# Seven-product units of a Hymba block: one of four column sums moved from VectorE to an adding transfer issued by GpSimd

## What is computed

```python
D_MODEL, SEQ, D_FF = 2048, 256, 5632
def swiglu(x, w_gate, w_up, w_down):
    return (jax.nn.silu(x @ w_gate) * (x @ w_up)) @ w_down
h = h + 1/2 * swiglu(rms_norm(h, ffn1_norm), w_gate1, w_up1, w_down1)
u = rms_norm(h, mix_norm) @ w_in          # split into attention and RWKV-7 columns
h = h + concat([dsa_attention(...), rwkv7_time_mix(...)]) @ w_out
h = h + 1/2 * swiglu(rms_norm(h, ffn2_norm), w_gate2, w_up2, w_down2)
return rms_norm(h, final_norm)
```

## Time and profile before

| what | value |
|---|---|
| median of 3 runs | 1834.93 us (1834.79 to 1837.94) |
| span of the profiled execution | 1834.2 us |
| median less that span | 0.7 us |
| TensorE busy | 1819.6 us, 99% |
| VectorE busy | 1505.4 us, 82% |
| ScalarE busy | 995.2 us, 54% |
| GpSimd busy | 11.1 us, 1% |
| HBM read | 360.19 MB |

### The profile page before, as it was taken

The page is one execution under the profiler, slowest core; times in us unless marked ns, Lnnn a source line. Parts: engine busy times, 40 slices in busy tenths (PEclk is TensorE's granted clock), DMA queues, the critical chain, the costliest instruction groups (busy, mean ns, idle before and its releaser), DMA issues. The chain is left out here.

```text
span 1834.2 us, 29749 instructions
## 1 busy us (share of the span) xinstructions
PE 1819.6 (99%) x10696; PEld 1546.4 (84%) x10696; DVE 1505.4 (82%) x1755; ACT 995.2 (54%) x1181; POOL 11.1 (1%) x23
## 2 busy tenths in 40 slices
PE   9999999999999999999999999999999999999998
PEld 7888888888888888999998878888888888888886
DVE  5888888888988985788867866688888888889996
ACT  7555555545555655754535655545555555555554
POOL 1000000000000000000000000000000000000000
PEclk9999999999999999999999999999999999999999
DMA  7677666777766778564443557677777677676664
GB/s 252 221 219 228 219 216 215 220 229 236 233 202 204 225 224 267 173 184 140 138 116 106 176 171 261 180 232 231 229 224 232 216 227 222 217 240 195 209 208 157
DMA packets 207851, 380.36 MB, mean 207 GB/s; under 512 B 16016, under 2 KB 35728, under 8 KB 207504
## 3 DMA queue, kind: packets, MB, share of 16 engines
q1 hardware_dynamic: 206768, 377.08, 65.7%
q10 hardware_dynamic: 480, 1.97, 0.3%
q0 software_dynamic: 512, 0.06, 0.0%
HBM read 360.19 MB, written 18.87 MB: 207 GB/s over the span
## 5 line engine op out<-in xcount | busy, mean ns | idle before, releaser
L402 ACT CAST whi<-raw 128x1024 fp32r<-128x1024 f32 (+1 forms) x648 | 675.1, 1047 | 700.8 <-DVE raw L1476 189.6
L411 DVE TENSOR_TENSOR wlo<-raw,whi 128x1024 fp32r<-128x1024 f32 (+1 forms) x648 | 771.7, 1212 | 208.4 <-ACT whi L402 194.5
L428 PE MATMUL psA<-whi,xh 128*128 128x512 f32 (+1 forms) x572 | 219.5, 384 | 0.5 <-DVE wlo L411 0.5
L428 PE MATMUL psA<-whi,xl 128*128 128x512 f32 (+1 forms) x572 | 219.2, 383 | 0.0
L428 PE MATMUL psA<-wlo,xh 128*128 128x512 f32 (+1 forms) x572 | 219.1, 383 | 0.0
L428 PE MATMUL psB<-whi,xh 128*128 128x512 f32 x544 | 211.7, 389 | 0.0
L428 PE MATMUL psB<-wlo,xh 128*128 128x512 f32 x544 | 211.6, 389 | 0.0
L428 PE MATMUL psB<-whi,xl 128*128 128x512 f32 x544 | 211.6, 389 | 0.0
L428 PEld LDWEIGHTS psA<-whi,xh 128*128 128x128 f32 x572 | 107.4, 188 | 21.6 <-DVE wlo L411 0.7
L428 PEld LDWEIGHTS psA<-whi,xl 128*128 128x128 f32 x572 | 107.4, 188 | 21.2
L428 PEld LDWEIGHTS psA<-wlo,xh 128*128 128x128 f32 x572 | 107.4, 188 | 21.0
(11 more groups left out here) (520 smaller groups left out, 3447.3 us busy)
## 6 DMA issues: line engine op xcount, KB each, us to landing
raw<-in_ffn_w_gate SPq DMA_DIRECT2D x176, 512.0 KB, 4.5
raw<-in_ffn_w_up SPq DMA_DIRECT2D x176, 512.0 KB, 4.6
raw<-in_ffn_w_down SPq DMA_DIRECT2D x176, 512.0 KB, 4.6
raw<-in_w_in SPq DMA_DIRECT2D x80, 512.0 KB, 3.6
raw<-in_w_out SPq DMA_DIRECT2D x32, 512.0 KB, 4.2
quads_dram<-stage SPq DMA_DIRECT2D x88, 128.0 KB, 4.2
stage<-quads_dram SPq DMA_DIRECT2D x22, 512.0 KB, 4.3
x<-in_x SPq DMA_DIRECT2D x4, 512.0 KB, 7.5
```

Source lines behind the costliest of these rows:

```text
L402: nc.scalar.copy(whi[:, slot, :, 0:ncol], raw[:, slot, :, 0:ncol]).then_inc(hi_ready, 1)
L411: nc.vector.tensor_tensor(wlo[:, slot, :, 0:ncol], raw[:, slot, :, 0:ncol], whi[:, slot, :, 0:ncol].bitcast(F32), ALU.subtract).then_inc(l ...
L428: mm = nc.tensor.matmul(ps[:, tb, 0:ncol], lhs[:, k0 + t, tok], rhs[:, slot, t, 0:ncol], start=(first and t == 0 and p == 0 and tb != open ...
```

## The change

In a unit the sum of the second group's halves is made by a transfer: GpSimd waits until the group has landed and issues a transfer that reads the group's second row tile from HBM once more and adds it, on its way, to the first half in `raw`. VectorE keeps three sums, formed in another order from that result. VectorE and ScalarE wait for the transfer with a new semaphore. To have that semaphore free, eight others of the mixing layer become two that count.

```diff
 # ScalarE, chunk and down
                     if kind == "unit":
                         unit = FIRST_UNIT[f] - GATE_UNITS + j
-                        nc.scalar.wait_ge(col_step, n * (4 * GATE_UNITS) + (4 * unit + 2))
+                        wait_summed(nc.scalar, n, unit)
                         split_hi(base, n, PER, g + 1)
                         unit_hi(n, unit)
...
+        def wait_summed(eng, n, unit):
+            eng.wait_ge(up_summed, n * (16 * GATE_UNITS) + 16 * (unit + 1))
+
+        def sum_rows(pool, n, unit, pair, w, col, base, per, g):
+            wait_raw(pool, base + g + 1, n, per)
+            if not (isinstance(n, int) and n * GATE_UNITS + unit == 0):
+                pool.wait_ge(up_summed, n * (16 * GATE_UNITS) + 16 * unit)
+            second = w[(pair * KT + 1) * P:(pair * KT + 2) * P, :]
+            pool.dma_start(raw[:, (base + g + 1) % SLOTS, 0, :], second[:, bass.ds(col, COLS)], accum_op=ALU.add)\
+                .then_inc(up_summed, 16)
...
         def unit_sums(base, n, per, g, unit, col_sum=col_sum):
-            steps = n * (4 * GATE_UNITS)
+            steps = n * (3 * GATE_UNITS)
             wait_raw(nc.vector, base + g, n, per)
-            wait_raw(nc.vector, base + g + 1, n, per)
...
-            tt(col_sum[:, 0, :], raw[:, gate, 0, :], raw[:, up, 0, :], ALU.add).then_inc(col_step, 1)
-            nc.vector.wait_ge(col_step, steps + (4 * unit + 1))
-            tt(raw[:, up, 0, :], raw[:, up, 0, :], raw[:, up, 1, :], ALU.add).then_inc(col_step, 1)
-            tt(col_sum[:, 1, :], col_sum[:, 0, :], raw[:, up, 1, :], ALU.add).then_inc(col_step, 1)
-            nc.vector.wait_ge(col_step, steps + (4 * unit + 3))
+            tt(col_sum[:, 1, :], raw[:, gate, 0, :], raw[:, up, 0, :], ALU.add).then_inc(col_step, 1)
+            nc.vector.wait_ge(col_step, steps + (3 * unit + 1))
+            tt(col_sum[:, 0, :], col_sum[:, 1, :], raw[:, up, 1, :], ALU.subtract).then_inc(col_step, 1)
             tt(col_sum[:, 2, :], col_sum[:, 1, :], raw[:, gate, 1, :], ALU.add).then_inc(col_step, 1)
...
 # VectorE, chunk and down
                     if kind == "unit":
+                        wait_summed(nc.vector, n, unit)
                         unit_sums(base, n, PER, g, unit)
...
+        def ffn_pool(pool, f, base, w_up, w_down):
+            def chunk(n):
+                for kind, j, g in chunk_items():
+                    if kind == "unit":
+                        sum_rows(pool, n, FIRST_UNIT[f] - GATE_UNITS + j, GATE_PAIR + j, w_up, n * COLS, base, PER, g)
+            chunk(1)
+            with pool.Fori(2, FC) as n:
+                chunk(n)
+            unit = FIRST_UNIT[f] + GATE_TOTAL
+            for m, kind, part, j, g in down_items(f):
+                if kind == "unit":
+                    sum_rows(pool, 0, unit, j, w_down, (2 * m + 1) * COLS, base + FC * PER, 0, g)
+                    unit += 1
...
 # GpSimd's list
+            ffn_pool(pool, 0, 0, *ffn1[1:])
             mix_pool(pool)
+            ffn_pool(pool, 1, base2, *ffn2[1:])
...
 # mixing layer: "exp0".."exp3" and "recip0".."recip3" become "exp" and "recip", waited for by level 1 to 4
```

More of the change, by code:

```diff
@@ L354, in build @@
         col_step = sem("col_step")
+        up_summed = sem("up_summed")
         col_hi_ready = sem("col_hi_ready")
@@ L758, in ffn_act @@
                 if kind == "unit":
-                    nc.scalar.wait_ge(col_step, 4 * unit + 2)
+                    wait_summed(nc.scalar, 0, unit)
                     split_hi(down, 0, 0, g + 1)
@@ L779, in unit_hi @@
         def unit_hi(n, unit, col_sum=col_sum):
-            nc.scalar.wait_ge(col_step, n * (4 * GATE_UNITS) + (4 * unit + 4))
+            nc.scalar.wait_ge(col_step, n * (3 * GATE_UNITS) + (3 * unit + 3))
             if not (isinstance(n, int) and n * GATE_UNITS + unit == 0):
@@ L980, in ffn_dve @@
                         nc.vector.wait_ge(unit_used, unit)
+                    wait_summed(nc.vector, 0, unit)
                     unit_sums(down, 0, 0, g, unit, col_raw)
@@ L1447, in build @@
             "kr_out", "k_roped", "qi_roped", "q_packed0", "q_packed1", "q0_roped", "q1_roped", "q_back0", "q_back1",
[2 rows of a table removed]
+            "scored0", "scored1", "scored2", "scored3", "max0", "max1", "max2", "max3", "exp",
+            "recip", "shares0", "shares1", "shares2", "shares3",
             "att_hi0", "att_hi1")}
@@ L1452, in build @@
         count = {}
+        counted = {f"{name}{n}": (name, n + 1) for name in ("exp", "recip") for n in range(4)}
         def done(ins, name):
-            if name in steps:
+            if name in counted:
+                ins.then_inc(steps[counted[name][0]], 1)
+            elif name in steps:
                 ins.then_inc(steps[name], 1)
@@ L1462, in need @@
         def need(eng, name):
-            eng.wait_ge(steps[name], 1)
+            name, level = counted.get(name, (name, 1))
+            eng.wait_ge(steps[name], level)
         def after(name):
-            if name in steps:
+            if name in counted:
+                nc.vector.wait_ge(steps[counted[name][0]], counted[name][1])
+            elif name in steps:
                 nc.vector.wait_ge(steps[name], 1)
```

## The result

The changed kernel takes 2174.57 us (median of 4 runs, 2166.64 to 2181.96) against 1835.76 on the same chip: 1.1845 times as long, with a 95% interval from 1.1814 to 1.1877, and 339 us more. The profiled execution took 2177.5 us, with a span of 2175.7. The forecast was 2055.

The account below looks back on a forecast made before the run. TensorE, busy 1819.6 of 1834.2 us, was taken to bound the kernel, with the new transfer making it wait. 1834.9 plus 100 (chunks) and 120 (down pairs) gave 2055 us, range 1915 to 2225.

Parts of the forecast that it names:

- last sign: Chunks: the forecast is wrong if TensorE's granted clock falls below 1.00 there.
- The price of L: Added transfer, all units: time from GpSimd's issue to landing, taken as 5.5 us.
- the forecast's two terms: Chunk units lose 20 x (2L - 6.0), 100 us; down pairs lose 29L - 39.5, 120 us.
- heavy rival: All units: L from 6.6 to 8 or over, 2131 to 2228 us, or TensorE's clock drops; chance 0.20.
- light rival: All units: L between 2 and 4.4, near the quiet 2.5 us row; 1868 us at 2.5, 1979 at 4.4; chance 0.17.
- Each step grows by L - 0.7: Down pairs: each 10.04 us step between units lengthens by L less the saved 0.7, to about 14.8 us.
- The term of 120: Down pairs: three pairs of 7 units and one of 8 lose 29L - 39.5, 120 us at L = 5.5.
- The rival's side remark: Down pairs: the cost of half-speed matmuls would hide in the loop; part of the rival with chance 0.20.
- The forecast's rule: Unit 1 of chunks: its own delay is L - 0.7, and TensorE waits for what exceeds the cover of 1.4 us.
- TensorE itself paces everything ahead of unit 0: Chunks: unit 0's cover of 3.2 us returns each chunk, so unit 1's 5.0 us wait recurs 20 times, 100 us.
- second half of the heavy rival: Chunks: clock drops, 21 matmuls behind each of 20 waits run at half speed; 95 us more, 2150 us; whole rival's chance 0.20.
- the likeliest case: Whole kernel: L from 4.4 to 6.6, likeliest 5.5, giving 2055 us; chance 0.60.

Follow-up runs that it names:

- The control: Changed kernel with no sum moved: VectorE makes all 69 sums itself, in the new order, with counted semaphores kept; 1835.39 us, 0.9999.
- The plain copies: Changed kernel with each adding transfer made a copy without the add: issued by GpSimd 2101.69 us, 1.1435; issued by ScalarE 2119.75 us, 1.1546.
- 8 KB: Changed kernel with the adding transfer covering only 16 of the 512 columns, still issued by GpSimd; 2059.71 us, 1.1201.
- the zeros: 22 zero matmuls ahead of TensorE's waits: changed kernel, FFN 1 only 2177.48 us, both networks 2158.57; kernel moving only unit 1 of chunks 1947.46.

## Why the prediction was right, and where it was not

**The direction and the main wait were right.** TensorE had nothing to give back and little cover; the landing of the second group was already the last thing a unit 1 waited for; a transfer behind it is paid by TensorE. The 0.7 us saved per unit show only as a part of each loop. The control says that the order of the sums, ScalarE's changed wait and the counted semaphores, which the forecast took to cost nothing, did cost nothing. GpSimd has no sum to wait for in it, so it says nothing of `mix_pool`'s place behind the sums; for that speaks the mixing layer, where TensorE works about as long as before (511.39 us against 510.26) in a stretch that is 3.9 us longer.

**The size was 119 us short**, 339 against 220. By its own last sign ("or if the granted clock falls below 1.00 in the chunks") the forecast is wrong: it fell to 0.93. The steps that failed:

*The price of L.* "I take 5.5" was 6.2 and 6.1. With these the forecast's two terms are 20 x (2 x 6.2 - 6.0) = 128 and 29 x 6.1 - 39.5 = 137, together 265: 45 us of the gap. The value was built from a load's 4.6 and 1.0 for GpSimd. The plain copies show that this 1.0 is not there in this place: 5.0 by GpSimd, 5.3 and 5.0 by ScalarE. What stood in the heavy rival's sentence ("because the transfer must also read what it adds to") has the right size, 1.1 to 1.2 us for the adding; whether it is that second reading isn't shown. One L for both places was a second simplification: with the means of 5.3 at unit 0 and 6.6 at unit 1 the first term is 20 x (5.3 + 6.6 - 6.0) = 118, 10 less. The light rival falls with its row of 2.5: even 8 KB take 4.3 to 4.5 here. The Trainium skill's fit (page "DMA: Bandwidth & Descriptors", section on the anatomy of a DMA on the SWDGE path), an estimated 2.6 us for this size, does not agree with the 5.0 of the plain copy. The Trainium skill, page "Collectives: The Full Stack", section on stop 4 (SDMA and CCE), says of collectives that the two reads and the write go "with the add free in between"; here, with a tile in SBUF as the target, the transfer with the add landed 1.1 to 1.2 us later than the copy and the kernel took 73 us more, and add and second reading cannot be told apart.

*What isn't in L.* The same two terms with the other kernels' L give 80 + 106 = 186 us for the plain copy (measured 265) and 60 + 85 = 145 for 8 KB (measured 223). So 74 to 79 us are missing at each measured price: the rule, and not only its L, was short. One part are two wake-ups that the forecast left out: L runs from GpSimd's issue to the landing, but before it GpSimd has to notice the load (landed at 214.59, instruction at 215.30: 0.7 us in the loop of the chunks, 0.28 in the down pairs), and after it VectorE has to notice the transfer (0.2 us in the chunks, 0.02 in the down pairs). That is 0.9 for each of 40 units and 0.3 for each of 29: 45 us by the forecast's own terms, in which each counts like L.

*Down pairs.* "Each step grows by L - 0.7" held: 10.04 - 0.7 + 6.1 = 15.4 with the measured price, and 15.15 were measured. The term of 120 became 150 in the kernel that moves only these, of which 29 x (6.1 + 0.3 - 5.5) = 26 are price and wake-ups. The rival's side remark, that a fallen clock would hide in this loop, held: with the zeros and a granted clock of 0.99 there, FFN 1's two pairs took 219.9 us, without them 220.3; FFN 2's took 229.9 and 232.4.

*Unit 1 of the chunks.* With unit 1 alone moved and the clock kept, the loss is 112 us, 5.6 a chunk. The forecast's rule gives L - 0.7 - 1.4 = 4.2 with that kernel's 6.3, and 5.1 with the 0.9 of the wake-ups: right to half a microsecond.

*"TensorE itself paces everything ahead of unit 0."* This is the step whose reason fell. By the forecast the cover of 3.2 us at unit 0 comes back in each chunk, and what exceeds it shows at unit 1. With unit 0 alone moved L was 5.1, so with the wake-ups 5.1 + 0.9 - 3.9 = 2.1 us would have passed on, and 1.4 of it been covered: 14 us in all. It was 45, and TensorE waited at unit 0 itself. The forecast never worked out TensorE's own cover there. In the kernel before it is 1.9 us: `col_lo` ends at 192.62 + 1.75 = 194.37, and TensorE, which starts the unit at 193.51, reads the column sums twelve matmuls later, at 196.2:

```profile
192.62 1.75 DVE L1476 TENSOR_TENSOR col_lo<-col_sum,col_hi 128x1536 fp32r<-128x1536 f32 x1
...
193.51 0.39 PE L439 MATMUL psT<-whi,xh 128*128 128x512 f32 x1
```

Nor does the cover ahead of VectorE come back whole. Counted from TensorE's start of the unit 1 before, over nine chunks of FFN 1, unit 0's second group landed at 20.1 us and VectorE came for it at 23.4; with unit 0 alone moved it lands at 21.3 and VectorE begins at 27.5. That is 4.1 us later, of which 0.7 are saved and 1.9 covered: 1.5 in each chunk, near the 1.32 that was measured as the wait. A late unit 0 makes unit 1's VectorE work late, that frees the slots later, and so the next chunk's unit 0 is loaded later: VectorE's sums, the slots, the loads and the transfer form a ring through all of a chunk, not only through the down pairs, and TensorE follows it. The kernels with zeros agree: faster matmuls made the chunk hardly shorter while unit 0 was in that ring, and by 1.7 us when it wasn't. TensorE is not out of that ring, though, since its regained speed brought the load of unit 0's second group forward by 1.1 us; why most of this was lost before the landing stays open. The 45 - 14 = 31 us here and the 45 of the wake-ups are, as an estimate, the 74 that no measured L gives; the parts are not independent, so the sum is no proof.

*The clock.* The second half of the heavy rival, 95 us for 20 waits at half speed, came true as an event and not as a price. The granted clock did fall, about once a chunk, in both networks, and the 20 steps behind unit 1's wait cost 2.1 to 2.5 us more each time, not 4.76, since it comes back after some ten matmuls. With the zeros 16 us of the time came back in this kernel; the rest is hidden.

So the likeliest case was right in where the time goes and in the band for L (4.4 to 6.6), and short in the sum. Its wait of about 5 us a chunk was 6.9, with unit 0's share (0.69 and 0.90) and unit 1's (6.39 and 5.88 in the two networks). That the time lies in the range is in part luck: with the measured L the forecast's sum is 1834.9 + 265 = 2100, and the time lies between the heavy rival's 2131 at L = 6.6 and 2228 at 8, though L itself is 6.2. The range was wide enough for a heavy transfer, and what filled it were wake-ups and a cover at unit 0 that the forecast had left out.

## What to carry to other kernels

A hand-over to a transfer costs the waker's time on both sides and the fixed part of the transfer, here over 5 us in all for 8 KB (4.5 and 0.9); put it only where the work behind it has that much room, and price it with a small transfer from the same queue under the same load, not from a quiet row. Ask of every cover whether it is refilled: where a handful of slots ties loads, splits and sums into a ring, a delay that fits the cover of the first pass may come back in each later one. And a fallen clock is no loss by itself: give the engine something to multiply in its waits and see whether the time moves, in the kernel and in a version without the suspected second wait.

## What was not expected of the hardware

- The adding of 256 KB in a transfer cost 1.1 to 1.2 us more than copying it (6.2 and 6.1 against 5.0 and 5.0). GpSimd's issuing instruction itself is longer, 864 ns against 537, and with 8 KB it is the same, 867.
- A plain 256 KB copy issued by ScalarE landed no sooner than GpSimd's (5.3 and 5.0 against 5.0 and 5.0). The Trainium skill, page "DMA: Bandwidth & Descriptors", section on latency and other measured facts, gives the first byte as coming after about 0.6 us on the path that ScalarE uses and about 1 us on GpSimd's, an estimated 0.4 us in favour of ScalarE; the landings here show nothing of it.
- The same adding transfer took 5.1 us where all were at unit 0 and 6.2 where all were at unit 1, and within the changed kernel 5.3 and 6.6 on average. At unit 1 stores and loads of SyncE stand close around it; that they are the cause was not tested.
- In FFN 1's chunk shown above TensorE did nothing from 238.6 to 246.09, and its granted clock was 0.50 from 243.70 to 250.50, which slowed some ten matmuls. With products of zeros in that wait it stayed at 1.00.
